# A decoder layer in fp32 split products: both feed-forward products as seven block products for eight

## What is computed

```python
def merge_and_ffn(x, y_ssm, y_attn, g_ssm, g_attn, w_ssm_out, w_attn_out, w_o, norm2_g, w_up, w_down):
    mix = jax.nn.sigmoid(g_ssm) * (y_ssm @ w_ssm_out) + jax.nn.sigmoid(g_attn) * (y_attn @ w_attn_out)
    x = x + mix @ w_o
    h = rms_norm(x, norm2_g)
    return x + jnp.square(jax.nn.relu(h @ w_up)) @ w_down
```

## Time and profile before

| | us |
|---|---|
| median of 3 runs | 1892.28 (1890.17 to 1895.39) |
| the profiled execution: span | 1890.3 |
| W_o block begins (first residual) | 1022.8 |
| the feed-forward block's first product | 1156.9 |
| TensorE busy | 1731.5 (92%) |
| VectorE, ScalarE, GpSimd busy | 898.4, 672.1, 487.9 |
| DMA | 135.22 MB, mean 72 GB/s |

### The profile page before, as it was taken

One profiled execution on the slowest core, in us unless ns is written; L12 is line 12 of the kernel. 1 busy time (PEld: TensorE's weight loads), 2 busy tenths in 40 slices (PEclk: granted clock), 3 DMA queues, 4 the chain that ended last, 5 costly groups with the idle time before them and its releaser, 6 DMA issues. The chain is left out here.

```text
span 1890.3 us, 29535 instructions
## 1 busy us (share of the span) xinstructions
PE 1731.5 (92%) x11464; PEld 1600.9 (85%) x11478; DVE 898.4 (48%) x1787; ACT 672.1 (36%) x1302; POOL 487.9 (26%) x295
## 2 busy tenths in 40 slices
PE   3989879977999988787799998999999999999999
PEld 2969539977999955555599987999999999999998
DVE  4850557898865537553343145333333333333334
ACT  5222445655433535442322245222222222222222
POOL 8211104875120000000643354111111112222100
PEclk9989989998999999999999998999999999999999
DMA  5122152212863114005552202111111111111102
GB/s 151 50 74 73 41 74 54 82 62 83 143 140 116 36 56 137 1 1 158 179 174 96 89 29 67 45 45 45 44 44 44 44 44 44 44 44 44 46 20 92
DMA packets 115446, 135.22 MB, mean 72 GB/s; under 512 B 17266, under 2 KB 95026, under 8 KB 115314
## 3 DMA queue, kind: packets, MB, share of 16 engines
q1 hardware_dynamic: 114578, 132.66, 24.6%
q0 software_dynamic: 480, 0.69, 0.2%
q10 hardware_dynamic: 288, 0.52, 0.1%
HBM read 109.67 MB, written 24.18 MB: 71 GB/s over the span
## 5 line engine op out<-in xcount | busy, mean ns | idle before, releaser
L2791 DVE TENSOR_TENSOR view_at<-psum,view_at 128x352 f32<-128x352 f32 x384 | 199.9, 524 | 154.1 <-PE psum L141 153.6
L139 PE MATMUL psum<-mix_hi,up_hi 128*128 128x352 f32 x768 | 249.4, 325 | 6.2 <-PEq L2355 6.2
L139 PE MATMUL psum<-hid_hi,dn_hi 128*128 128x352 f32 x768 | 249.8, 325 | 0.0
L140 PE MATMUL psum<-mix_lo,up_hi 128*128 128x352 f32 x768 | 247.2, 322 | 0.0
L140 PE MATMUL psum<-hid_lo,dn_hi 128*128 128x352 f32 x768 | 247.1, 322 | 0.0
L141 PE MATMUL psum<-mix_hi,up_lo 128*128 128x352 f32 x768 | 247.1, 322 | 0.0
L141 PE MATMUL psum<-hid_hi,dn_lo 128*128 128x352 f32 x768 | 246.3, 321 | 0.0
L139 PE MATMUL psum<-h_hi,w_hi 128*128 128x352 f32 x600 | 196.7, 328 | 21.7 <-POOL w_lo L211 19.6
L2782 DVE TENSOR_TENSOR hid_lo<-psum,hid_hi 128x352 fp32r<-128x352 f32 x96 | 50.3, 524 | 326.7 <-ACT hid_hi L2743 326.7
L140 PE MATMUL psum<-h_lo,w_hi 128*128 128x352 f32 x600 | 194.9, 325 | 0.0
L141 PE MATMUL psum<-h_hi,w_lo 128*128 128x352 f32 x600 | 194.5, 324 | 0.0
(11 more groups left out here) (383 smaller groups left out, 3580.2 us busy)
## 6 DMA issues: line engine op xcount, KB each, us to landing
view_at<-w_in SPq DMA_DIRECT2D x18, 1024.0 KB, 5.5
view_at<-w_up SPq DMA_DIRECT2D x16, 1024.0 KB, 5.6
view_at<-w_down SPq DMA_DIRECT2D x16, 1024.0 KB, 4.8
gate_dram<-view_at SPq DMA_DIRECT2D x48, 176.0 KB, 2.0
view_at<-gate_dram SPq DMA_DIRECT2D x16, 528.0 KB, 4.5
view_at<-cache_k SPq DMA_DIRECT2D x32, 256.0 KB, 3.4
view_at<-cache_v SPq DMA_DIRECT2D x32, 256.0 KB
out<-view_at SPq DMA_DIRECT2D x34, 128.0 KB, 1.7
```

The source lines that it names most:

```text
L139: nc.tensor.matmul(out, lhs[0], rhs[0], start=start, stop=False)
L140: nc.tensor.matmul(out, lhs[0], rhs[1], start=False, stop=False)
L2791: nc.vector.tensor_tensor(x, psum[:, 4 + j % 4, 0:TH], x, ALU.add).then_inc(add_done, 1)
```

## The change

The 2x2 block form of a product needs 7 block products in place of 8 when sums of blocks are multiplied (`PROD`: the seven pairs and the accumulator of each). The up product splits channels in and tokens in half and pairs of 128 hidden channels; the down product splits the hidden channels, model channels and tokens. A block product of an up chunk is now 24 matmuls of 264 tokens (`TQ`), accumulators are pairs of PSUM banks of 528 tokens (`TF`), and products with `start` false go on top of an earlier one's sum.

- W_o is made in 32 units of 264 tokens (24 matmuls each), and x + mix @ w_o is also stored to DRAM (`x1_dram`).
- The normalised x (4 blocks) gives seven blocks, each split into high and low part (`high_b`, `low_b`, 4 pieces of 528 columns each), by ScalarE, VectorE and GpSimd. The first 8 products (`EJ`: P1 and P2 of chunks 0 to 3) need only blocks of the first half of the tokens.
- Up: 16 chunks of 7 products. Per chunk VectorE makes 4 sums of weight blocks (`sums_u`, 512 columns), 5 sums of accumulators (`sum_y`, `sum_z`, `sum_21`, `sum_12`, 528) and 4 sums of relu blocks (`sums_h`, 528). ScalarE does 4 relus, 4 squares, 7 high parts of weights, 1 copy. GpSimd does 7 low parts (512). The seven blocks (270 KB each) are stored to `hid_dram`.
- Down comes after all of up: 8 groups of 7 products, 48 matmuls of 264 each, in 4 units (`mt`) of 12. Each product loads its block of hidden values from DRAM (540 KB), ScalarE makes two high parts (1056 and 1024 columns), GpSimd the weights' low part (1024), VectorE the hidden low part (`low_d`, 1056), 4 `drain`s (528) out of PSUM into SBUF, and per group 4 sums of weight blocks (`sums_d`, 1024).
- The two blocks of the program are one, without the barrier; loops are written out. `turn_back` stands between whole products at the end, in four rounds of 5 pieces.

The core of the diff (of the removed code only the order of the feed-forward's products is shown):

```diff
+    B11, B21, B22, T2, T1, T3, T4 = range(7)
+    A11, A12, A22, S1, S2, S3, S4 = range(7)
+    X, Y, Z, W = range(4)
+    PROD = {1: (A11, B11, X), 2: (A12, B21, X), 3: (S4, B22, W), 4: (A22, T4, Z),
+            5: (S1, T1, W), 6: (S2, T2, Y), 7: (S3, T3, Z)}
+    FIRSTS = (1, 5, 6, 7)
...
+    NE = 4
+    EJ = [(0, 1), (1, 1), (0, 2), (1, 2), (2, 1), (3, 1), (2, 2), (3, 2)]
+    ERANK = (0, 2, 1, 3, 4, 6, 5, 7)
+    UJ = list(EJ)
+    for c_ in range(NCH):
+        UJ += [(c_, p_) for p_ in ((6, 5, 7, 4, 3) if c_ < NE else (1, 6, 5, 7, 2, 4, 3))]
...
+                if c == LASTC:
+                    sp.wait_ge(up_mm, at_u(c, 1) + 1)
+                    load_x1(0)
+                    sp.wait_ge(up_mm, at_u(c, 6) + 1)
+                    load_raw_d(0)
+                    load_raw_b(0)
+                    load_raw_b(1)
...
+            sp.wait_ge(su_done, 4 * NCH)
+            sp.wait_ge(ua_lo, U_END)
+            load_raw_b(2)
+            for j, buf in ((T1, T1s), (T2, T2s), (T3, T3s), (T4, T4s)):
+                sp.wait_ge(ts_done, 4 * LASTC + (T1, T2, T3, T4).index(j) + 1)
+                store_h(LASTC, j, buf)
+            sp.wait_ge(up_mm, U_END)
+            load_raw_d(1)
+            for j in range(7):
+                sp.wait_ge(h_st[j], 16 * (NCH - (NE if j == B11 else 0)))
+            for j in (2, 1, 3):
+                load_x1(j)
+            for n in range(3, ND):
+                sp.wait_ge(db_lo, n - 2)
+                load_raw_b(n)
+                d, i = divmod(n, 7)
+                if i == 6 and d + 2 < ND_:
+                    sp.wait_ge(sd_done, 4 * (d + 1))
+                    sp.wait_ge(da_lo, 7 * d + 5)
+                    load_raw_d(d + 2)
...
+            def unit(n):
+                c, q, z = OJ[n]
+                if n >= 4:
+                    pe.wait_ge(x1_done, n - 3)
+                for k in range(KD):
+                    if q == 0 and z == 0 and k % (KD // 2) == 0:
+                        pe.wait_ge(wo_lo_done, 2 * c + k // (KD // 2) + 1)
+                    f, cols = slice(P * z, P * (z + 1)), slice(TQ * q, TQ * (q + 1))
+                    last = split_mm(psum[:, n % 4, 0:TQ], (woh[c % 2][:, k, f], wol[c % 2][:, k, f]),
+                                    (mixT[0][:, k, cols], mixT[1][:, k, cols]), k == 0, k == KD - 1)
+                last.then_inc(mm_done, 1)
...
+            def total(q):
+                pe.wait_ge(acc_done, LAST_SQ[q])
+                if q >= 2:
+                    pe.wait_ge(mean_done, q - 1)
+                nc.tensor.matmul(psum[:, 6 + q % 2, 0:TQ], ones, acc[:, q, :], start=True, stop=True).then_inc(sum_done, 1)
...
+                elif p == 4:
+                    pe.wait_ge(u3_done, c + 1)
+                elif p == 3:
+                    pe.wait_ge(c22_done, c + 1)
+                s = slot_u(n)
+                for u in range(2):
+                    for k in range(KH):
+                        cols = slice(TQ * u, TQ * (u + 1))
+                        last = split_mm(psum[:, 2 * b + u, 0:TQ], (s[0][:, k, :], s[1][:, k, :]),
+                                        (bh[j][:, k, cols], bl[j][:, k, cols]),
+                                        p in FIRSTS and k == 0, k == KH - 1, p not in FIRSTS)
...
+            def down(n, mt):
+                d, p = DJ[n]
+                j = n % SLOTS
+                if mt == 0:
+                    pe.wait_ge(da_lo, n + 1)
+                    pe.wait_ge(db_lo, n + 1)
+                if n:
+                    pe.wait_ge(drained, 4 * (n - 1) + mt + 1)
...
+            for i in range(16):
+                unit(2 * i)
+                if i in RESID:
+                    residual(RESID[i])
+                if i == 12:
+                    total(0)
+                elif i == 13:
+                    total(1)
+                elif i == 15:
+                    total(2)
+                unit(2 * i + 1)
+            up(0)
+            total(3)
+            for n in range(1, NU):
+                up(n)
+            for n in range(ND - 2):
+                for mt in range(4):
...
+            n = ND - 2
+            pe.wait_ge(drained, 4 * n)
+            for i in range(5):
+                turn_back(0, i, i)
+            for mt in range(4):
+                if mt < 3:
+                    pe.wait_ge(y_done, (2, 4, 5)[mt])
+                down(n, mt)
+            n += 1
+            pe.wait_ge(drained, 4 * n - 1)
...
+                if i == 14:
+                    root(1)
...
+                        act.wait_ge(scaled_q, 2)
+                    for k in range(KH):
+                        high_b(B11, k, h2(0, 0, k))
+                square(2 * i)
+                square(2 * i + 1)
...
+                if i == 14:
+                    for k in range(KH):
+                        high_b(B21, k, h2(1, 0, k))
+                    high_u(1)
+                    high_u(3)
+                    root(2)
+            high_u(4)
+            high_u(6)
+            copy_p1(0)
+            root(3)
+            copy_p1(1)
+            high_u(5)
+            high_u(7)
+            square_11(2)
+            for k in range(KH):
+                act.wait_ge(t_sum[1], k + 1)
+                high_b(T2, k, t2raw[:, k, :])
+            square_11(3)
+            for k in range(KH):
+                act.wait_ge(t_sum[0], k + 1)
+                high_b(T1, k, h2(0, 0, k))
+            copy_p1(4)
+            for k in range(KH):
+                act.wait_ge(t_sum[2], k + 1)
+                high_b(T3, k, h2(0, 1, k))
+            copy_p1(5)
+            high_u(8)
+            high_u(9)
+            square_11(6)
+            for k in range(KH):
+                high_b(B22, k, h2(1, 1, k))
+            square_11(7)
+            for k in range(KH):
+                act.wait_ge(t_sum[3], k + 1)
+                act.wait_ge(up_mm, len(EJ))
+                high_b(T4, k, h2(1, 0, k))
+            for n in range(10, len(EJ) + RING):
+                high_u(n)
...
+            def sum_z(c):
+                dve.wait_ge(up_mm, at_u(c, 7) + 1)
+                dve.wait_ge(u2_done, c + 1)
+                if c:
+                    dve.wait_ge(c22_done, c)
+                v.tensor_tensor(two(u3), pair(Z), two(u2), ALU.add).then_inc(u3_done, 1)
+                dve.wait_ge(u3_done, c + 1)
+                v.tensor_tensor(pair(Y), pair(W), two(u3), ALU.add).then_inc(c22_done, 1)
...
+                dve.wait_ge(h12, c + 1)
+                if c < NE:
+                    dve.wait_ge(b11_in, 16 * (c + 1))
+                else:
+                    dve.wait_ge(h11, c + 1)
+                if c:
+                    for j in (T1, T2, T3, T4):
+                        dve.wait_ge(h_st[j], 16 * c)
+                v.tensor_tensor(T1s, C12s, C11s, ALU.subtract).then_inc(ts_done, 1)
+                dve.wait_ge(h22, c + 1)
+                dve.wait_ge(ts_done, 4 * c + 1)
+                v.tensor_tensor(T2s, C22s, T1s, ALU.subtract).then_inc(ts_done, 1)
+                v.tensor_tensor(T3s, C22s, C12s, ALU.subtract).then_inc(ts_done, 1)
+                dve.wait_ge(h21, c + 1)
+                dve.wait_ge(ts_done, 4 * c + 2)
+                v.tensor_tensor(T4s, C21s, T2s, ALU.subtract).then_inc(ts_done, 1)
...
+            def drain(n, mt):
+                d, p = DJ[n]
+                to = {1: U2a, 2: CA[X], 6: U2a, 7: c22, 4: CA[Z], 5: c22, 3: CA[W]}[p][:, mt, :]
+                dve.wait_ge(dn_mm, 4 * n + mt + 1)
+                if n == 0:
+                    v.tensor_copy(two(to), pair(mt)).then_inc(drained, 1)
+                    return
+                if d == 0 and mt == 0 and p in (2, 7, 4, 3):
...
+                    dve.wait_ge(u2_added, 1)
+                if n == ND - 2:
+                    if mt == 0:
+                        dve.wait_ge(u2_added, 3)
+                    x = CA[W][:, mt, :]
+                    v.tensor_tensor(two(x), pair(mt), two(x), ALU.add).then_inc(last_w, 1)
+                if n == ND - 1 and mt == 0:
+                    dve.wait_ge(last_w, 4)
+                v.tensor_tensor(two(to), pair(mt), two(to), ALU.add).then_inc(drained, 1)
...
+            def add_u2(x):
+                for mt in range(4):
+                    ins = v.tensor_tensor(x[:, mt, :], x[:, mt, :], U2a[:, mt, :], ALU.add)
+                ins.then_inc(u2_added, 1)
+            for n in range(len(OJ)):
+                if n in (26, 28):
+                    mean((n - 26) // 2)
+                if n == 28:
+                    scale(0)
+                if n == 30:
+                    scale(1)
                 add(n)
-            dve.wait_ge(x1_done, len(OJ) - 6 + 2)
-            mean(0)
-            add(len(OJ) - 3)
-            scale(0)
...
+                if p == 6:
+                    sum_y(c)
+                    if c + 1 < NCH:
+                        sums_u(c + 1, 1)
+                if p == (6 if c < NE else 1) and c:
+                    sums_h(c - 1)
+                if p == 5 and c + 1 < NCH:
```

(37 more changed lines are left out.)

1021 lines of the change are left out of this document (649 added, 372 removed).

## The result

The kernel after takes 1900.4 us (median of 20 runs, 1893.5 to 1907.5), the kernel before 1893.3 in the same sessions (20 runs, 1888.5 to 1897.9). The ratio is 1.0041, 95% interval 1.0031 to 1.0051: 7 us slower, which is more than the 0.3% that can be told from no change. The forecast was 1890, some 2 us faster than before, with a range of 1862 to 1916: the time lies in the range, and on the other side of no change.

The account below looks back on a forecast made before the run. TensorE's matmul count and cost bound the last 867.5 us; -72.5 for matmuls, -11.9 and -3.0 for old stops, +28.5, +13, +23.5, +7 and +13 for new waits gave -2.4, so 1890 us, range 1862 to 1916.

Parts of the forecast that it names:

- the price of the slow clock behind TensorE's stops: After a stop TensorE runs at 1.2 GHz for a while; some 1.5 us lost each time.
- Matmuls: W_o, up and down: 6144 matmuls of 264 columns at 122.1 ns, 750.2 us, which is 72.5 us less.
- Rival (d): TensorE's price for 264 columns is set by weight loads, so the saving shrinks; 1%.
- first products: End of W_o and start of up: TensorE waits for sums, copies and low parts; +28.5 us with four slow-clock spells.
- P4 of three chunks: Chunks 1 to 3 of up: this product waits for `sum_z`, 4 us each; +13 us with some slow clock.
- transition: Up to down: TensorE idles 0.5, 8 and 12 us for drains and a late relu block; +23.5 us with two slow spells.
- in down: Down products: a drain comes 1 us late only where S1, S2 are summed, 7 times; +7 us.
- end: Last group of down: late drains stop TensorE 1.4 and 6.1 us, rounds of transposes 3; +13 us in all.
- some 50 to 60 us idle: Sign expected in the profile if right: TensorE's idle time after 1022.8 us.
- (a): Start, chunks, transition, end: small waits mostly vanish and the saving shows, 58 us for 85, 1863 us; 32%.
- (b): VectorE bounds the down product, `low_d` waiting for GpSimd; up to 72 us, half of it gives 1926; 15%.
- (c): Up chunks: stores to DRAM don't overlap, 22.4 against 20.5 us, 23 us over 12 chunks, 1913; 7%.

Follow-up runs that it names:

- e4_trans: Kernel after with SyncE's queue reordered between up and down, relu blocks ahead of the down weights and x1: 1882.9 us.
- e5_tail: Kernel after with the two groups of adds `add_u2` moved from behind the fourth-last product's drains to behind the third-last's: 1890.9 us.
- e3_sumz: Kernel after with VectorE forming the previous chunk's four relu sums after `sum_z` instead of before it in chunks 1 to 3: 1882.8 us.
- e2_train: Kernel after with ScalarE taking chunk 2's and 3's first products out earlier, and S1 and S2 with their parts ahead of T2's and T3's low parts: 1899.1 us.
- e10_low2: Kernel after with one more VectorE subtraction of 1056 columns in each down product from the thirteenth on: 1954.9 us.
- e8_all: Kernel after with five reorderings together (`total(2)`, first chunks, `sum_z`, up to down, the end): 1855.9 us, 0.9798 of the kernel before.
- e1_total2: Kernel after with the third row of sums, `total(2)`, issued after W_o's last unit instead of before it: 1891.3 us.

## Why the prediction was wrong

The step that failed is the price of the slow clock behind TensorE's stops. The forecast added 11.5 us for it and took 3.0 off for the old spells, 8.5 net; the traces have 19.8. The 11.3 us between turned 2 us faster into slower. The work was forecast well, and the stops in their sum.

**Matmuls.** -72.5 forecast, and 1 more for the eight added transposes and the last store; -72.7 measured for all of the work. 122.1 ns per matmul forecast, 121.1 and 122.1 measured. Rival (d) is out.

**Where TensorE stops.** All stops named came, in their places and with their releasers. Their sizes, forecast and measured: first products 22.5 (6.2, 5.1, 5, 3, 3 and gaps) and 27.8, where the wait for `copy_p1(4)` was 9.30 instead of 5; P4 of three chunks 12 and 14.2; transition 20.5 (0.5, 8, 12) and 22.7 (5.12, 4.70, 12.92); in down 7 and 1.5; end 10.5 (1.4, 6.1 and 3 for the rounds) and 5.9. Together 72.5 and 72.1, with errors of 5 us either way that cancel, which is luck. In the transition the first relu blocks come 5 us late behind the weights, which I had not seen. With them ahead (`e4_trans`) the first two stops are 0.42 and 6.15 in place of 5.12 and 4.70, so they cost 3.3 us, and the 8 forecast for the second was too much.

**The clock is the term that failed.** Forecast: four slow spells at 1.5 us each at the start (6), "some slow clock" (1 us) for the chunks, two spells (3) in the transition, one (1.5) at the end. Measured in the same places: 6.9, 7.5, 5.2 and 2.1, which is 21.7; 2.6 more lie in W_o's first 6 us, where the kernel before has such a spell too (1.5). More than half of the miss is P4 of chunks 1 to 3, 1 us forecast and 7.5 measured. Two things were off, about equally. The count: no spell was booked in full for the three stops at P4, though they were forecast at 4 us each and the old ones of 5.7 and 6.2 had one each; all three had one, and the transition had three for two. And how much of a spell TensorE works through. The old spell behind the barrier, first, those at P4 of the kernel after, then those at P4 in the trace of `e5_tail` (each window lies just inside a spell; behind its length TensorE's busy us, and the granted clock is the third number from the end):

```profile
1153.70:1160.50 6.80, 3.64 (x12) 3.67 (x13) 2.10 (x4) 4.56 (x8) 3.50 (x3) 0.50 0.00 1
```

```profile
1222.80:1229.50 6.70, 5.93 (x27) 5.96 (x28) 2.82 (x5) 2.36 (x4) 2.56 (x2) 0.50 0.22 83
1243.30:1250.00 6.70, 4.57 (x21) 4.60 (x22) 3.90 (x5) 2.35 (x4) 2.76 (x3) 0.50 0.36 134
1267.20:1273.90 6.70, 6.06 (x27) 6.09 (x28) 2.20 (x4) 1.72 (x3) 1.28 (x1) 0.50 0.22 83
```

```profile
1210.40:1213.70 3.30, 2.80 (x13) 2.83 (x14) 2.26 (x3) 2.12 (x4) 1.60 (x2) 0.50 0.24 90
1230.90:1234.20 3.30, 2.77 (x12) 2.81 (x13) 2.29 (x3) 2.15 (x4) 1.58 (x2) 0.50 0.25 92
1251.40:1258.10 6.70, 4.95 (x22) 4.98 (x23) 2.92 (x5) 1.72 (x3) 1.28 (x1) 0.50 0.30 111
```

All but two of these spells are 6.8 us long. In the first, TensorE stood still until 1156.86, so it worked 3.64 us at half clock and lost the 1.6 that the forecast took as the price of any spell. The spells at P4 begin 0.7 to 2.2 us before the stop ends; TensorE works 4.6 to 6.1 us of each and loses 2.1 to 2.7. `e3_sumz` shows this term alone: with the stops at 0.9 to 2.6 the clock is 1.00 through and 7 of the 16 us come from it. A second trace with nearly the same stops as after (`e2_train`, 72.4 us idle) lost 24.6 to the clock, so the size isn't one execution's.

**The sum.** -2.4 forecast, +6.2 measured: +11.3 for the clock (19.8 for 8.5), -1.5 for the stops (59.1 for 72.5 less 11.9), -1.2 for the work (-72.7 for -71.5). The "some 50 to 60 us idle" of the forecast's last part contradicts its own terms, which are 72.

**Rivals.** (a), small waits vanish: no, except in the down product, where 7 us were booked and 1.5 came, and at the end (5.9 for 10.5); in the other places the idle time is above the forecast, not below. (b), VectorE bounds the down product: not in the kernel after, whose `low_d` has a mean of 2.05 us for 1.26 alone, so it waits 0.8 us and not the 2.4 of the rival; but `e10_low2` shows the edge right behind it. (c), stores that don't overlap: none of it in chunks 4 to 15, 826 matmuls in 100 us at 144 GB/s. The row that the forecast set against it was misread: the stretch of the earlier trace rows at over 340 GB/s holds two loads of 1 MB (W_o's and the up weights') beside those of 128 KB, so it doesn't show the rate of small transfers by themselves. That VectorE and GpSimd exclude each other held: after, GpSimd's low part of 1024 columns has a mean of 2.85 us (2.39 in the earlier trace rows), and VectorE's drains from PSUM stay at 0.69 to 0.71:

```profile
L3264 DVE TENSOR_TENSOR view_at<-psum,view_at x220: 689/695/710, 1557.5 to 1895.5; 128x528 f32<-128x528 f32 x110
...
L3216 DVE TENSOR_TENSOR db_lo<-view_at,db_hi x56: 1241/2055/3460, 1523.0 to 1863.4; 128x1056 fp32r<-128x1056 f32 x56
```

What stays open: why the same stop is followed by a long spell in one execution and a short one in another (below), and so how much of the last us of the sum is luck of one trace.

## What to carry to other kernels

A change that saves work everywhere and adds dependences at the seams is paid at the seams: here 72.7 us of work were bought with 59 us of waiting in four places and 20 us of slow clock behind it, and reordering queues there (relu blocks ahead of weights, the sum that TensorE waits for ahead of those that are only stored) gave 44 us back without touching the arithmetic. Price a stop of TensorE as its length plus the slow matmuls behind it, and read from whole spells in the trace how much of each TensorE works through: 3.6 to 6.1 us of the 6.8 in the rows above. And before handing a part of VectorE's work to GpSimd, look whether VectorE's operations there read PSUM; with both inputs in SBUF the two together (8.9 us) were slower than VectorE alone (8.0).

## What the runs showed of the hardware

A matmul of 264 columns is 121 to 122 ns from the next at the full clock and 220 ns at a granted clock of 0.50 (starts of 1225.03 and its neighbours), which is 264 columns at 1.2 GHz with nothing added; the some 12 ns beside the columns are there at full clock only. The loss at the lower level is thus 0.45 of the busy time for this size. The Trainium skill ("TensorE: Matmul & The Clock Gate", Terms) gives the penalty as the time at the lower level times one half. The traces don't agree: from W_o on after has 85.2 us at 0.50 and `e8_all` 37.5, which would be 42.6 and 18.8 and leave 759 and 773 us for the same work. Only 54 of the 85.2 us are busy, and with 0.45 of the busy time, 24.3, the rest above comes out equal to 1.2 us in after and nine variants (`e10_low2`, with its many stops, has 783.9). Idle time at the lower level costs nothing.

The three stops at P4 (4.1 to 5.8 us in every trace without the new order) have a spell each in every such trace. In those of after and `e2_train` all three are 6.8 us long; in those of `e1_total2`, `e4_trans` and `e5_tail` two of the three are 3.4 us. The loss there is 4.9 to 7.5 us. So what a stop costs in clock is not fixed by its length alone, and a single trace's clock term is uncertain by some 3 us at this place.
